# A hybrid encoder layer on one core: Fourier transforms in pieces between the projection's blocks, and the final norm during the last expert's down projection

## The chip, the cores and the metric

The kernel is one program on 1 core of one Trainium2 chip. The metric is the device time of one execution in microseconds; lower is better. A core has five engines with their own instruction streams: TensorE (PE; PEld is its weight load), VectorE (DVE), ScalarE (ACT), GpSimd (POOL) and SyncE (SP). They are ordered by semaphores alone. SP and POOL also issue the DMAs, which move data between main memory and the on-chip memory.

## The reference

Two batches of rows go through the same layer, 1024 rows ("prompt") and 256 ("sample"), each of width 1024. The kernel stacks them to T = 1280 rows, ten tiles of 128.

```
h = rmsnorm(x, norm_mix);  u = h @ w_in                 # w_in is 1024 x 2048
u_b, u_c, u_x, u_f = split(u)                           # 512 columns each
y_conv = rmsnorm(u_b * conv3(u_c * u_x), g_conv)        # 3 taps along the rows
y_four = rmsnorm(real(fft2(u_f over rows and over groups of 64 columns)), g_fourier)
x = x + concat(y_conv, y_four) @ w_out                  # 1024 x 1024
h = rmsnorm(x, norm_ffn)
aff = softmax(h @ w_router);  each of 16 experts takes its top rows (128 prompt, 32 sample)
ye = (silu(h_e @ w_gate[e]) * (h_e @ w_up[e])) @ w_down[e] * gate   # hidden width 2816
x[rows of e] += ye
out = rmsnorm(x, norm_final)
```

All of it is float32. Most products are made of three matmuls: each operand is split into a high part (rounded) and a low remainder, and high x high, high x low and low x high are added.

## The kernel before

**Projection.** Each 128-row tile of x is squared and summed (ACT, L566), scaled by its norm (DVE, L795), turned by TensorE (L1140), and split into `hT_h` (ACT, L576) and `hT_l` (DVE, L803). When all ten tiles are there, 16 blocks of 128 output columns follow. A block loads 128 columns of `w_in` (SP), scales and splits them into `win_h` (ACT, 8 instructions, L586) and `win_l` (DVE, 8 instructions, L810), and runs 72 matmuls (L1150) into one of two sets of three PSUM banks. The order is 12 blocks for the convolution and then 4 for the Fourier half. A block's consumer frees its banks for the block after the next.

**Fourier half.** After each of its four blocks ACT copies the second half of the rows (L612), DVE makes sums and differences (`tc`, L854), and both are split into `AB_h` (L615) and `AB_l` (L856). After the last block come "channels": per row tile 12 matmuls against the table `dd`, and a split of the 1024 columns into `Y_h` (ACT, L624) and `Y_l` (DVE, L865). Then come the "waves", for j = 0 to 3: 24 matmuls for the even frequencies, 24 for the odd ones and 12 for the sample rows, against the tables `tab_h`, `tab_l`, `tsm`. ACT copies the sines (`qcp`, L642), and DVE adds and subtracts (`yfour`, L883 to L895). `w_out` is loaded and split in halves of its rows' tiles between the waves, through two small buffers `wo_raw` (L632, L873). POOL squares and adds for the norms.

**Rows.** For each of the ten tiles `half` runs 24 + 24 matmuls with the two halves of `w_out`; DVE adds them to x, the norm is taken, and the router's logits are made. Results go to `acc_dram` (x) and `xn_dram` (its norm). Top-k runs on DVE beside and behind it. After `routed` POOL gathers the first expert's rows.

**Experts.** Weights come in 33 units of 1 MB per expert (22 for gate and up, 11 for down) through 11 slots. ACT writes `spl_h` (L704) and DVE `spl_l` (L1060) three units ahead of TensorE; a unit of the prompt is 12 matmuls. Sample rows are multiplied unsplit at five places of an expert (L1336, L1344), the last two behind the 7th and the 11th down unit. At an expert's end ACT scales the results by the gate (`yP`, `yS`), and POOL adds them into `acc_dram` by an indirect DMA.

**Final norm.** After the last expert all ten tiles are read from `acc_dram` (L461), normed (ACT L780 and L782, DVE L1126 and L1128) and written (L464).

The order is written out by hand in each engine's stream; an engine takes its instructions strictly in that order. The lines above are those of the profile.

Of the kernel before, what the change touches and what calls it, by code (L numbers as in the profile page):

```python
# [19 lines left out]
P = 128  # L20
# [8 lines left out]
E = 16  # L29
# [31 lines left out]
HALF = SEQ // 2  # L61
GROUPS = ((0, 4), (4, 8), (8, TILES))
EARLY = 4
# [8 lines left out]
def build(nc, x, norm_mix, w_in, conv_w, g_conv, g_fourier, w_out, norm_ffn, w_router, w_gate, w_up, w_down,  # L72
# [8 lines left out]
    out_t = out.rearrange("(t p) d -> t p d", p=P)  # L81
    win_v = w_in[0].rearrange("(k p) e -> p k e", p=P)

    win_v2 = w_in[0].rearrange("(k p) (a j l c) -> j p k a l c", p=P, a=4, j=2, l=2)
# [5 lines left out]
    with ExitStack() as ctx:  # L90
# [13 lines left out]
        Y_h = at("Y_h", 0, [P, JH, TILES, 2 * P], F32R)  # L104
        Y_l = at("Y_l", 40 * KB, [P, JH, TILES, 2 * P], F32R)
        yconv = at("yconv", 80 * KB, [P, JH, T])
        AB_h = at("AB_h", 100 * KB, [P, JH, T], F32R)
        AB_l = at("AB_l", 120 * KB, [P, JH, T], F32R)
# [11 lines left out]
        uc = at("uc", 164 * KB, [P, T])  # L120
        v = at("v", 169 * KB, [P, VW])
        tc = at("tc", 175 * KB, [P, T + 2])
        qc = at("qc", 181 * KB, [P, T])
        sqc = at("sqc", 186 * KB, [P, T])

        woc_h = at("woc_h", 140 * KB, [P, JH, D], F32R)
        woc_l = at("woc_l", 156 * KB, [P, JH, D], F32R)
        tab_h = at("tab_h", 172 * KB, [P, HB, LARGE], F32R)
        tab_l = at("tab_l", 172 * KB + HB * LARGE * 4, [P, HB, LARGE], F32R)
        tsm = at("tsm", 100 * KB, [P, 2, SMALL], F32R)  # L130
        qf = at("qf", 103 * KB, [P, T])
        sqf = at("sqf", 108 * KB, [P, T])
        qcp = at("qcp", 113 * KB, [P, HE + HO + SE + SO])
        wo_raw = at("wo_raw", 116 * KB, [P, 2, DH])

        wof_h = at("wof_h", 0, [P, JH, D], F32R)
# [10 lines left out]
        A0 = at("A0", 100 * KB, [E, HALF])  # L147
        A1 = at("A1", 102 * KB, [48, HALF])
        v0 = at("v0", 104 * KB, [E, CAP])
        v1 = at("v1", 104 * KB + 512, [48, CAP])  # L150
        i0 = at("i0", 105 * KB, [E, CAP], U32)
        i1 = at("i1", 105 * KB + 512, [48, CAP], U32)
        i0f = at("i0f", 106 * KB, [E, CAP])
        i1f = at("i1f", 106 * KB + 512, [48, CAP])
# [57 lines left out]
        def bank(b, n=1):  # L212
            return psf[:, b * 512:(b + n) * 512]

        const_in = sem("const_in")
        gffn_in = sem("gffn_in")
        dd_in = sem("dd_in")
        tab_in = sem("tab_in")
# [1246 lines left out]
```

## Time and profile before

| | us |
|---|---|
| median of 3 runs | 2580.14 (2579.91 to 2581.01) |
| the profiled execution's own time | 2579.22 |
| its span, first to last instruction | 2577.3 |
| TensorE busy in the span | 2438.6 (95%) |
| VectorE busy | 1650.2 (64%) |
| ScalarE busy | 1344.1 (52%) |
| GpSimd busy | 194.7 (8%) |
| mean granted clock of TensorE | 0.972 of full speed |

Full speed of TensorE is 2.4 GHz; the other level is half of that. All times in the text are positions or lengths within the span. The busy share alone does not tell what a stage is worth: 2438.6 of 2577.3 us are busy, and what can be won without fewer matmuls lies in the idle stretches and in those at the lower clock.

### The profile page before, as it was taken

The page shows a single profiled execution, that of the slowest core. Times are in us where ns is not written, and L with a number is a line of the kernel's source. Part 1 is how long each engine was busy: PE and PEld are TensorE (multiplying, and loading weights), DVE is VectorE, ACT ScalarE, POOL GpSimd, SP SyncE. Part 2 cuts the span into 40 slices and gives each one's busy share as a digit, 9 for nine tenths or more (in the row PEclk, how much of TensorE's full clock was granted, in tenths as well). Part 3 has the DMA queues.
Part 4 walks back from the last instruction along what each step waited for, and adds up shares of the span by engine and source line. Part 5 has one row for each costly group of instructions (what it writes and reads, how often), then busy time and mean ns, then how long its engine had stood idle before and what let it go on. Part 6 is the DMA issues. An engine that isn't in the chain of part 4 may idle for free.

```text
span 2577.3 us, 45156 instructions
## 1 busy us (share of the span) xinstructions
PE 2438.6 (95%) x18269; PEld 1915.0 (74%) x18269; DVE 1650.2 (64%) x1350; ACT 1344.1 (52%) x1233; POOL 194.7 (8%) x191
## 2 busy tenths in 40 slices
PE   5999879759999999999999999999999999999994
PEld 4888768647777777777777777777777777777773
DVE  4344455967676767667676666676767676666674
ACT  5222322325555556556555555565656565556563
POOL 0010120010101010101010101001010101010000
PEclk8999889879999999999999999999999999999997
DMA  3110242426878786868787878787877878787866
GB/s 119 41 33 25 99 168 107 173 98 258 317 264 316 269 299 262 298 261 299 279 305 280 307 280 307 279 309 269 313 275 285 301 264 322 266 320 267 318 261 222
DMA packets 296891, 627.28 MB, mean 243 GB/s; under 512 B 21392, under 2 KB 72848, under 8 KB 296464
## 3 DMA queue, kind: packets, MB, share of 16 engines
q1 hardware_dynamic: 288336, 598.88, 63.1%
q0 software_dynamic: 8384, 25.71, 3.7%
q8 instruction: 157, 2.57, 0.4%
q14 instruction: 14, 0.11, 0.0%
HBM read 598.31 MB, written 26.21 MB: 242 GB/s over the span
## 4 chain that ended last, share of the span: by engine, by line
PE 90%; DVE 5%; DMA 2%; ACT 1%; issue 1%; SPq 0%; POOL 0%; DVEq 0%; ACTq 0%; POOLq 0%
PE ps L353 20%; PE ps L354 19%; PE ps L355 19%; PE ps L1336 12%; PE ps L1150 9%; PE ps L1344 6%; PE ps L1354 1%; DVE i L935 1%; DVE v L933 1%; DVE A L937 1%; DMA raw<-in_w_gate_dram 1%; PE ps L1295 1%; DMA wo_raw<-in_w_out_dram 1%; DVE wof_l L873 0%; PE ps L1363 0%
## 5 line engine op out<-in xcount | busy, mean ns | idle before, releaser
L1060 DVE TENSOR_TENSOR spl_l<-raw,spl_h 128x2048 fp32r<-128x2048 f32 x528 | 1209.3, 2292 | 553.5 <-ACT spl_h L704 548.4
L704 ACT ACTIVATE spl_h<-raw 128x2048 fp32r<-128x2048 f32 x528 | 1012.1, 1917 | 576.5 <-PE ps L355 447.3
L353 PE MATMUL ps<-spl_h,xT 128*128 128x512 f32 x1408 | 555.0, 394 | 3.2 <-DVE xT L1065 2.5
L354 PE MATMUL ps<-spl_l,xT 128*128 128x512 f32 x1408 | 549.8, 390 | 0.0
L355 PE MATMUL ps<-spl_h,xT 128*128 128x512 f32 x1408 | 548.8, 390 | 0.0
L353 PEld LDWEIGHTS ps<-spl_h,xT 128*128 128x128 f32 x1408 | 264.7, 188 | 78.8 <-issue 22.3
L1336 PE MATMUL ps<-raw,xTs 128*32 128x256 f32 (+1 forms) x6144 | 314.2, 362 | 0.0
L355 PEld LDWEIGHTS ps<-spl_h,xT 128*128 128x128 f32 x1408 | 264.8, 188 | 56.1
L354 PEld LDWEIGHTS ps<-spl_l,xT 128*128 128x128 f32 x1408 | 264.8, 188 | 53.3
L353 PE MATMUL ps<-spl_h,g 128*128 128x512 f32 x704 | 278.0, 395 | 0.0
L354 PE MATMUL ps<-spl_l,g 128*128 128x512 f32 x704 | 274.4, 390 | 0.0
L355 PE MATMUL ps<-spl_h,g 128*128 128x512 f32 x704 | 274.3, 390 | 0.0
L1336 PEld LDWEIGHTS ps<-raw,xTs 128*32 128x32 f32 x6144 | 189.4, 110 | 109.7 <-issue 8.1
L538 POOL DMA_INDIRECT acc_dram<-yP,sidx x16 | 26.7, 1669 | 1797.1 <-ACT yP L745 1797.1
L353 PEld LDWEIGHTS ps<-spl_h,g 128*128 128x128 f32 x704 | 132.1, 188 | 40.0 <-issue 13.2
L1344 PE MATMUL ps<-raw,gs 128*32 128x256 f32 x2816 | 158.6, 380 | 0.0
L355 PEld LDWEIGHTS ps<-spl_h,g 128*128 128x128 f32 x704 | 132.2, 188 | 28.2
L354 PEld LDWEIGHTS ps<-spl_l,g 128*128 128x128 f32 x704 | 132.2, 188 | 26.6
L1344 PEld LDWEIGHTS ps<-raw,gs 128*32 128x32 f32 x2816 | 88.2, 110 | 63.3 <-issue 8.3
L1150 PE MATMUL ps<-hT_h,win_h 128*128 128x512 f32 (+1 forms) x384 | 96.6, 360 | 5.9 <-DVE win_l L810 5.9
L1150 PE MATMUL ps<-hT_l,win_h 128*128 128x512 f32 (+1 forms) x384 | 96.3, 359 | 0.0
L1150 PE MATMUL ps<-hT_h,win_l 128*128 128x512 f32 (+1 forms) x384 | 96.2, 359 | 0.0
(199 smaller groups left out, 1961.5 us busy)
## 6 DMA issues: line engine op xcount, KB each, us to landing
raw<-in_w_up_dram SPq DMA_DIRECT2D x352, 512.0 KB, 8.3
raw<-in_w_gate_dram SPq DMA_DIRECT2D x352, 512.0 KB, 9.6
raw<-in_w_down_dram SPq DMA_DIRECT2D x176, 1024.0 KB, 14.9
win_raw<-in_w_in_dram SPq DMA_DIRECT2D x16, 512.0 KB, 3.8
xt<-in_x_dram SPq DMA_DIRECT2D x10, 512.0 KB, 8.3
xr<-in_x_dram SPq DMA_DIRECT2D x10, 512.0 KB, 4.0
acc_dram<-xr SPq DMA_DIRECT2D x10, 512.0 KB, 2.6
xn_dram<-xn SPq DMA_DIRECT2D x10, 512.0 KB, 2.9
```

What stands on the lines that cost most here:

```text
L353: eng.matmul(o, a_h, b_h, start=first, stop=False, skip_group_check=True)
L354: eng.matmul(o, a_h, b_l, start=False, stop=False, skip_group_check=True)
L355: return eng.matmul(o, a_l, b_h, start=False, stop=last, skip_group_check=True)
L538: pool.indirect_dma_start(acc, bass.IndirectOffsetOnAxis(sidx[:, 0:1], 0), yP[:, :], None, compute_op=ALU.add).then_inc(added[0], 16)
L704: act.activation(spl_h[:, i % SPL, :], raw[:, slot_of(i), :], ACT.Copy).then_inc(sh_ok, 1)
L933: dve.max(v[0:n, rs], A[0:n, :]).then_inc(top_ok[h], 1)
L935: dve.max_index(idx[0:n, rs], v[0:n, rs], A[0:n, :]).then_inc(top_ok[h], 1)
L937: dve.match_replace(A[0:n, :], v[0:n, rs], A[0:n, :], -2.0).then_inc(top_ok[h], 1)
L1060: dve.tensor_tensor(spl_l[:, i % SPL, :], raw[:, slot_of(i), :], spl_h[:, i % SPL, :].bitcast(F32), ALU.subtract).then_inc(sl_ok, 1)
L1150: last = pe.matmul(u[:, t0:t1], w[:, slot, k, :], h[:, k, t0:t1], start=(k == 0 and i == 0), stop=(k == KD - 1 and i == 2), skip_group_che ...
L1336: last = pe.matmul(o, xTs[:, k, :], v_, start=k == 0, stop=k == KD - 1, skip_group_check=True)
L1344: last = pe.matmul(bank(6)[q * CAPS:(q + 1) * CAPS, 0:DQ], gs[:, f, :], raw[:, slot_of(i), b * D + q * DQ:b * D + (q + 1) * DQ], start=f = ...
```

## The change

1. **The start.** SP issues x's first tile and the weights of block 0 ahead of the small constants. The blocks are reordered: the four Fourier blocks are 0 to 3, the twelve convolution blocks 4 to 15. Blocks 0 and 1 run in pieces of rows (0:512, 512:1024, 1024:1280), and TensorE turns tiles 4 to 9 between their matmuls.
2. **Fourier pieces.** After the eight steps k of block n, TensorE runs `waves` of Fourier block n-3 (k = 0, 1, 2) and `channels` of block n-2 (k = 3 to 7). `Y` and `AB` shrink to what one or two blocks need. ACT and DVE work through the same loop over n. The tables are loaded at the start.
3. **w_out** is loaded whole: its first half during blocks 10 to 14, its second half after step 3 of block 15.
4. **Norm sums.** POOL makes the squares and sums of the Fourier half after block 6, TensorE sums them in block 10; ACT makes the squares of the convolution half.
5. **Experts' first loads.** Three units instead of four are loaded ahead of the rows; unit 7 and those behind it wait for `routed`. The first gather reads `idxT` directly, without the two copies into `gidx`.
6. **The final norm.** During the last expert's down projection all rows are read from `acc_dram` (which holds experts 0 to 14), normed and written to `out`, through five buffers and POOL's queue. The last expert's own rows are gathered ahead (`accP`, `accS`), get its result, are normed and overwrite their rows in `out` by two indirect DMAs at the end.

The core of the diff:

```diff
+FX = 5
+NORMS = {INS + 2: (0,), INS + 3: (1,), INS + 4: (2,), INS + 5: (3,), INS + 6: (4,), INS + 8: (5,), INS + 9: (6, 7),
+         INS + 10: (8, 9)}
-EARLY = 4
+EARLY = 3
...
 # SP
+            sp.dma_start(xt[:, 0, :], x_t[0]).then_inc(x_in[0], 16)
+            load_win(0)
+            for t in range(1, 5):
+                sp.dma_start(xt[:, t, :], x_t[t]).then_inc(x_in[t], 16)
+            load_win(1)
...
+            sp.wait_ge(hT_half, 1)
+            for k in range(JH):
+                sp.dma_start(wof_raw[:, k, :], wout_v[JH + k]).then_inc(wof_in[k // 2], 16)
...
             for i in range(EARLY, UNITS):
+                if slot_of(i) == 4:
+                    sp.wait_ge(routed, 1)
...
 # POOL, end
+            pool.wait_ge(xg_ps, E)
+            for t in range(3):
+                load_rows(t)
+            pool.wait_ge(pe_s, (E - 1) * SAMPLE + NC)
+            for t in range(3, FX):
+                load_rows(t)
+            for t in range(2):
+                store_rows(t)
+            for t in range(2, TILES):
+                if t + 3 < TILES:
+                    pool.wait_ge(f_out[(t + 3) % FX], 16)
+                    load_rows(t + 3)
+                store_rows(t)
+            for s in range(FX):
+                pool.wait_ge(f_out[s], 16 * len(range(s, TILES, FX)))
+            pool.wait_ge(z_ok, 1)
+            pool.indirect_dma_start(out, bass.IndirectOffsetOnAxis(sidx[:, 0:1], 0), accP[:, :], None).then_inc(z_out, 16)
+            pool.wait_ge(z_ok, 2)
+            pool.indirect_dma_start(out_q, bass.IndirectOffsetOnAxis(sidx[:, 1:2], 0), accS[:, :], None).then_inc(z_out, 16)
...
 # ACT
+            for n in range(1, PROJ):
+                if n <= JH:
+                    halves(n - 1)
...
+                if n + 1 < PROJ:
+                    win_hi(n + 1)
+                if n <= JH:
+                    sums_hi(n - 1)
...
+                if 3 <= n < 3 + JH:
+                    sines(n - 3)
+                if 2 <= n < 2 + JH:
+                    channels_hi(n - 2)
...
+            def row_norm(t):
+                act.wait_ge(f_in[t % FX], 16 * (t // FX + 1))
+                act.activation(bank(4, 2), fx[t % FX][:, :], ACT.Square, accum_out=fss[:, t:t + 1]).then_inc(fs_ok, 1)
+                act.wait_ge(fs_ok, t + 1)
+                act.activation(fss[:, TILES + t:TILES + t + 1], fss[:, t:t + 1], ACT.Sqrt, bias=eps[:, 0:1],
+                               scale=1.0 / D).then_inc(frt_ok, 1)
...
 # DVE, in expert(e, last), and behind the last expert
+                    if last:
+                        if i == 0:
+                            adder()
+                        for t in NORMS.get(i, ()):
+                            row_scale(t)
...
+            for k, (ps_, rows_, gain) in enumerate(((bank(0, 2), accP, gfin), (bank(6)[:, 0:DQ], accS, gfinq))):
...
+                dve.scalar_tensor_tensor(out=rows_[:, :], in0=ps_, scalar=cgate[:, k:k + 1], in1=rows_[:, :],
+                                         op0=ALU.mult, op1=ALU.add).then_inc(z_sum, 1)
+                dve.wait_ge(z_rt, k + 1)
+                dve.reciprocal(zrr[:, k:k + 1], zrt[:, k:k + 1]).then_inc(z_rr, 1)
+                dve.wait_ge(z_rr, k + 1)
+                dve.scalar_tensor_tensor(out=rows_[:, :], in0=rows_[:, :], scalar=zrr[:, k:k + 1], in1=gain[:, :],
+                                         op0=ALU.mult, op1=ALU.mult).then_inc(z_ok, 1)
...
 # PE
+            project(0, 0, 512, more_x({1: 4, 4: 5}))
+            pe.wait_ge(winl_ok, 2)
+            project(1, 0, 512, more_x({1: 6, 4: 7, 7: 8}))
+            pe.wait_ge(hTl_ok, 8)
+            project(0, 512, 1024, more_x({2: 9}))
+            pe.wait_ge(hTl_ok, 9)
+            project(1, 512, 1024)
+            pe.wait_ge(hTl_ok, TILES)
+            project(0, 1024, T)
+            project(1, 1024, T)
...
+            def posts(n):
+                def after(k):
+                    if 3 <= n < 3 + JH and k < 3:
+                        waves(n - 3, k)
+                    if 2 <= n < 2 + JH and k >= 3:
+                        channels(n - 2, k - 3)
+                    if n == 10 and k == 3:
+                        pe.wait_ge(qf_ok, 1)
+                        norm_sums(qf, 16)
+                return after
```

`row_scale(t)` is a reciprocal and one scaling on DVE, as L1126 and L1128 were; `adder` builds a 128 x 128 matrix of 32 x 32 identities, with which one matmul adds the four quarters of a sample row's sum of squares. In the order lists below, "waits" names the semaphores.

TensorE behind the last projection block, before:

```order
L1150 MATMUL ps<-hT_h,win_l 128x512 x2
L1150 MATMUL ps<-hT_h,win_l 128x256
L1180 MATMUL ps<-ones,qc 128x1 [waits q_ok]
L1180 MATMUL ps<-ones,qc 128x1 x9
L353 MATMUL ps<-dd,AB_h 128x256 [waits abl_ok,dd_in]
L354 MATMUL ps<-dd,AB_h 128x256
L355 MATMUL ps<-dd,AB_l 128x256
```

TensorE of the change, where block 2 ends and block 3 begins (`dd` is a channels piece, `tab` a piece of waves):

```order
L380 MATMUL ps<-dd,AB_l_56 128x256
L1297 MATMUL ps<-hT_h,win_h 128x512 [waits ab_ok,winl_ok]
L1297 MATMUL ps<-hT_h,win_h 128x512
L1297 MATMUL ps<-hT_h,win_h 128x256
L1297 MATMUL ps<-hT_l,win_h 128x512 x2
L1297 MATMUL ps<-hT_l,win_h 128x256
L1297 MATMUL ps<-hT_h,win_l 128x512 x2
L1297 MATMUL ps<-hT_h,win_l 128x256
L378 MATMUL ps<-tab_h,Y_h 128x258 [waits tab_in,Yl_ok]
L379 MATMUL ps<-tab_l,Y_h 128x258
```

The pieces stood behind all blocks; now each stands behind 9 of a block's 72 matmuls.

VectorE in block 3 of the change, up to the first waves:

```order
L918 TENSOR_TENSOR sums<-ps,tmp 128x512 [waits abl_ok,tmp_ok]
L918 TENSOR_TENSOR sums<-ps,tmp 128x512
L918 TENSOR_TENSOR sums<-ps,tmp 128x128 x2
L891 SCALAR_TENSOR_TENSOR win_l<-win_raw,gmix,win_h 128x128 [waits winh_ok]
L891 SCALAR_TENSOR_TENSOR win_l<-win_raw,gmix,win_h 128x128 x7
L922 TENSOR_TENSOR AB_l_56<-sums,AB_h_54 128x1280 [waits abh_ok]
L937 TENSOR_TENSOR yfour<-ps,qcp 128x257 [waits qcp_ok]
L938 TENSOR_TENSOR yfour<-ps,qcp 128x255
```

Before, the `yfour` pair stood behind the channels' splits alone; now a block's sums and weight split stand ahead of it.

VectorE in the last expert's down projection, before:

```order
L1060 TENSOR_TENSOR spl_l<-raw,spl_h 128x2048 [waits sh_ok] x7
L1088 TENSOR_TENSOR g<-ps,g 128x4x128 [waits gh_ok]
L1060 TENSOR_TENSOR spl_l<-raw,spl_h 128x2048 [waits sh_ok]
L1126 RECIPROCAL frr<-fss 128x1 [waits frt_ok,gfin_in]
L1128 SCALAR_TENSOR_TENSOR fo<-fx,frr,gfin 128x1024 [waits fr_ok]
```

And in the change (`fx_125` and `fx_126` are two of the five row buffers):

```order
L1180 TENSOR_TENSOR spl_l<-raw,spl_h 128x2048 [waits sh_ok]
L1214 RECIPROCAL frr<-fss 128x1 [waits frt_ok]
L1216 SCALAR_TENSOR_TENSOR fx_125<-fx_125,frr,gfin 128x1024 [waits fr_ok]
L1180 TENSOR_TENSOR spl_l<-raw,spl_h 128x2048 [waits sh_ok]
L1208 TENSOR_TENSOR g<-ps,g 128x4x128 [waits gh_ok]
L1214 RECIPROCAL frr<-fss 128x1 [waits frt_ok]
L1216 SCALAR_TENSOR_TENSOR fx_126<-fx_126,frr,gfin 128x1024 [waits fr_ok]
```

A row tile's scaling now stands between two splits of weights.

## Rows read from the trace of the kernel before

**Rows 1.** Windows: length, busy time (instructions) by engine, granted clock, DMA share, GB/s

```profile
43.44:270.77 227.33, 227.33 (x1155) 192.95 (x1155) 84.44 (x159) 49.76 (x129) 21.09 (x8) 0.99 0.11 33
270.77:301.39 30.62, 19.77 (x139) 18.34 (x138) 15.55 (x16) 12.44 (x14) 3.03 (x4) 0.87 0.44 164
301.39:351.57 50.18, 33.32 (x240) 32.42 (x241) 32.02 (x50) 15.91 (x34) 19.57 (x8) 0.81 0.33 107
...
2541.40:2577.30 35.90, 0.00 (x0) 0.00 (x0) 13.76 (x20) 15.31 (x32) 1.55 (x1) 0.56 0.90 325
```

**Rows 2.** Timeline of the start: start, length, engine, line, output and inputs, count

```profile
4.08 5.13 SPq L370 DMA_DIRECT2D xt<-in_x_dram  x10
...
22.91 1.02 ACT L576 ACTIVATE hT_h<-ps 128x1024 fp32r<-128x1024 f32 x1 [0.48 <-PE ps L1140]
...
31.31 1.09 PE L1140 MATMUL ps<-ident,xs 128*128 128x128 f32 x8 [0.91 <-DVE xs L795]
...
38.55 4.76 ACT L586 ACTIVATE win_h<-win_raw,gmix 128x128 fp32r<-128x128 f32 x16
...
41.11 4.43 DVE L810 SCALAR_TENSOR_TENSOR win_l<-win_raw,gmix,win_h 128x128 fp32r<-128x128 f32 x16 [1.20 <-ACT win_h L586]
```

**Rows 3.** Chain of waits, 270 to 360 us: start, length, what

```profile
271.57 1.70 DVE tc L854 x4
273.29 1.28 ACT AB_h L615
274.59 1.50 DVE AB_l L856
...
307.04 0.40 ACT qcp L642
307.46 0.43 DVE yfour L883
...
358.69 2.12 PE ps L1180 x20
```

**Rows 4.** Timeline of TensorE: first matmuls of two neighbouring sets of waves

```profile
310.87 0.37 PE L353 MATMUL ps<-tab_h,Y_h 128*128 128x258 f32 x1
...
317.90 0.37 PE L353 MATMUL ps<-tab_h,Y_h 128*128 128x258 f32 x1
```

**Rows 5.** Windows, a stretch during the waves, columns as in Rows 1

```profile
326.00:331.00 5.00, 5.00 (x30) 5.00 (x31) 5.00 (x4) 1.08 (x3) 4.90 (x2) 0.66 0.32 102
```

**Rows 6.** TensorE's waits from 270 to 352 us: total, times, longest

```profile
PE ps L353 <- DVE Y_l L865: 3.2, 4, 0.8
```

**Rows 7.** Timeline around the first gather

```profile
533.42 2.26 POOL L518 COPY gidx<-idxT 128x1 uint32<-128x1 uint32 x1 [179.19 <-DVE gateT L1055]
...
543.85 1.94 PE L1295 MATMUL ps<-ident,xg 128*128 128x128 f32 x8 [10.90 <-DMA xgs<-xn_dram,gidx]
```

**Rows 8.** Timeline of VectorE and ScalarE in the last down projection

```profile
2516.35 2.29 DVE L1060 TENSOR_TENSOR spl_l<-raw,spl_h 128x2048 fp32r<-128x2048 f32 x1 [0.42 <-ACT spl_h L704]
...
2517.12 1.92 ACT L704 ACTIVATE spl_h<-raw 128x2048 fp32r<-128x2048 f32 x1 [0.80 <-PE ps L355]
```

**Rows 9.** Chain of waits, 2500 us to the end

```profile
2520.40 6.18 PE ps L1344 x112
...
2542.66 5.27 DMA acc_dram<-yS,sidx
...
2555.47 1.16 ACT fsq L780 x2
2556.65 0.30 ACT fss L782
2557.17 1.28 DVE fo L1128
```

**Rows 10.** Transfers: count, KB each, median us from issue to landing

```profile
tsm<-in_dft_s_dram POOLq DMA_DIRECT2D x1, 260.0 KB, 4.0
...
xgs<-xn_dram,gidx POOLq DMA_INDIRECT x16, 7.7
```

More of the change, by code:

```diff
@@ new lines, in wo_lo @@
+            def wo_lo(n):
+                dve.wait_ge(woh_ok, n + 1)
+                k = n % JH
+                full, hi, lo = ((woc_raw, woc_h, woc_l) if n < JH else (wof_raw, wof_h, wof_l))
+                dve.scalar_tensor_tensor(out=lo[:, k, :], in0=full[:, k, :], scalar=gm2[:, n:n + 1],
+                                         in1=hi[:, k, :].bitcast(F32), op0=ALU.mult, op1=ALU.subtract).then_inc(wol_ok, 1)
+            for n in range(1, PROJ):
+                if n <= JH:
+                    sums_of(n - 1)
+                j, q = divmod(n - 1 - JH, 3)
+                if n > JH and q == 1:
+                    gated(j)
+                if n > JH and q == 2:
+                    conv_out(j)
+                if n + 1 < PROJ:
+                    win_lo(n + 1)
+                if n <= JH:
+                    sums_lo(n - 1)
+                if n > JH and q == 1:
+                    taps(j)
+                if 3 <= n < 3 + JH:
+                    waves(n - 3)
+                if 2 <= n < 2 + JH:
+                    channels_lo(n - 2)
+                if n == 11:
+                    dve.wait_ge(rn_rt, 1)
+                    dve.reciprocal(rn[:, 1, :], rm[:, 1, :]).then_inc(rn_a, 1)
+                if n == 14:
+                    for k in range(JH):
+                        wo_lo(k)
@@ L1184, in _ @@
[L1184 to L1195 removed]
+                    if n == PROJ - 1 and k == JH - 1:
+                        last.then_inc(hT_half, 1)
@@ new lines, in project, with channels @@
+                    if k == KD - 1 and t1 == T:
+                        last.then_inc(u_done, 1)
+                    if between is not None:
+                        between(k)
+            def channels(j, p):
+                if p == 0:
+                    pe.wait_ge(abl_ok, j + 1)
+                    if j:
+                        pe.wait_ge(yf_ok, 8 * j)
+                    else:
+                        pe.wait_ge(dd_in, 16)
+                if p >= 2:
+                    pe.wait_ge(Yl_ok, PIECES * j + p - 1)
+                for i in range(2):
+                    ts = slice((2 * p + i) * P, (2 * p + i + 1) * P)
+                    last = three(pe, bank(6 + p % 2)[:, i * 2 * P:(i + 1) * 2 * P], AB_h[j % 2][:, ts], AB_l[j % 2][:, ts],
@@ L1410, in _ @@
             expert(E - 1, True)
+            pe.wait_ge(same_ok, 2 * QS - 2)
+            pe.wait_ge(z_sq, 2)
+            pe.matmul(bank(7)[:, 0:1], same[:, :], zss[:, 1:2], start=True, stop=True).then_inc(z_ps, 1)
 def split12(a):
```

672 lines of the change are left out of this document (362 added, 310 removed).

## The prediction

> **What bounds the kernel now.** I read the windows by stage first, then the chain of waits where a window shows idle time, then the timeline there for durations. The windows [rows 1] show four kinds of stage. The 16 projection blocks run without a gap, 227.3 us or 14.2 a block, with VectorE and ScalarE at 84 and 50 us. The channels (30.6 us) have TensorE busy 19.8 us, and the waves with the loading of `w_out` (50.2 us) 33.3 us, at a granted clock of 0.87 and 0.81. After the last matmul 35.9 us pass without TensorE. The stage of the rows, the top-k and experts 0 to 14 are the same work in both kernels. So three places count: the start and Fourier half (0 to 351.6 us), the first gather, and the end. The total matmul work stays.
>
> **The start.** x's first tile is issued at 4.08 us [rows 2]; with only one small transfer ahead it goes out near 1.3, 2.8 us earlier. ScalarE then makes block 0's `win_h` ahead of the tiles: half of 4.76, 2.4 us [rows 2], which gives that back. Tile 3's `hT_h` ended at 23.9 us; it stays near 23.6, and VectorE, with half of 4.43 us for `win_l`, about 1.5 of it in idle time, ends tile 3's `hT_l` near 26.5. There the first projection piece starts, instead of at 43.4. Blocks 0 and 1 are 28.2 us of matmuls (227.3 less about 2 for the slow beginning, over 16: 14.08 a block), the six tiles turned between them take 1.1 us each at the high clock [rows 2], 7 with their hand-offs, and the slow first microseconds cost 1.7, as a first run of matmuls does here: both end near 63.4.
>
> A wait is added: block 2's `win_h` needs block 0 finished, and block 0 ends only 2.8 us (24 matmuls of 256 columns at 0.118) ahead of block 1. From 60.6 on: ScalarE's copy of halves 0.8, `win_h` 2.4, `win_l` 2.2, hand-offs 0.4. Block 2 starts at 66.5; TensorE stands 3 us.
>
> **The Fourier pieces.** From 66.5: 14 blocks at 14.08 are 197.1; channels, 120 matmuls at 0.12, are 14.4; waves, four sets at 7.03 (310.87 to 317.90) [rows 4], are 28.1; one norm sum is 2.1 [rows 3]. What each piece waits for follows from the hand-offs, in block 3 counted from its first matmul. ScalarE ends the last channels copy at 0.7, the halves at 1.5, `win_h` at 3.9, `AB_h` (1.28) at 5.2, and then takes the sines (0.40). VectorE ends the sums (1.70) at 3.2, `win_l` at 6.2, `AB_l` (1.50) at 7.8, and the first `yfour` pair (0.43 and 0.33) at 8.6 [rows 3]. TensorE comes to the second waves piece at 1.76 + 2.95 + 1.76 = 6.5, so it waits 2.2 us. All behind that is covered: the third piece's needs are ready 1 us early, and a channels piece has 1.76 us of matmuls against 1.3 of splitting. The same in block 4; 0.9 us in block 5, which has no sums; 2.6 in block 6, where the gated product and taps stand ahead. Together 7.9 us. Queued behind the waiting matmul are only the block's own; nobody else is late, since blocks 3 to 5 last 25 to 27 us and the other engines need under 14.
>
> Do these waits cost clock? Four waits of 0.8 us in the channels [rows 6] left the clock high, but a stretch of the waves with single waits around 1 us in it shows 0.66 [rows 5]. The bounds are 0 and one slow stretch behind each of five waits at 1.7, 8.5 us; I take 4.6, half way.
>
> Block 15 ends at 66.5 + 197.1 + 14.4 + 28.1 + 2.1 + 7.9 + 4.6 = 320.7. Then VectorE's last convolution product, the copy of the first row tile and its low part, 3.5 us: `half` starts at 324.2. Before it started at 351.57 [rows 1]. Gain 27.4 us. `w_out`'s transfers and splits are off the path: 2 MB are issued 7 us ahead, and the second half's splits (8.1 us on ScalarE behind block 15) end before `half`, the norm sum and their 3.5 us are over at 12.7. Bounds: 18 (all waits double, clock lost at each) and 37 (no wait, no clock lost).
>
> The Trainium skill has a rule on this tail. "SBUF — State Buffer", section Who interferes with whom, says that a VectorE instruction with two inputs in this memory blocks a GpSimd instruction that reads it, and the other way round, for its whole length. GpSimd's last sum of squares would by it stand against the splits of `w_out` behind block 15. By the rule one of them is up to 3 us later, still inside the 12.7; the sum would lose 0 to 1 us. The next paragraph's rows agree with the rule.
>
> **The first gather.** GpSimd copies two index columns at 533.42, 2.26 us each, and TensorE gets its rows at 543.85 [rows 7]. The change drops both copies, 4.5 us, and a hand-off of 0.9. But four units, 4 MB, are now requested at that very moment; under such load the second gather takes 7.7 us to land [rows 10], against about 3.7 here (10.4 us from 533.42 to 543.85, less 4.5 and 0.9, less 1.3 until the second of two gathers is issued). 5.4 less 4.0 is 1.4; without any collision 5.4. I take 3. Unit 7 is split only after four units' work; its 4 MB are in 15 us after the request: no wait.
>
> **The end.** In the last down projection a unit lasts 2.72 us; ScalarE works 1.92 and idles 0.80, VectorE 2.29 and idles 0.42 [rows 8]. A row tile adds 1.16 + 0.30 + 0.1 on ScalarE and 1.28 + 0.17 + 0.15 on VectorE [rows 9]. VectorE then needs 3.9 us a unit over five units, TensorE 2.72. The three split buffers give 1.1 us of lead and TensorE stops behind the 7th down unit for the sample rows' 6.18 us [rows 9]: following units 3 to 7 through, TensorE loses 1.05 us once and catches the rest there. The transfers are free, as all weights are in by then.
>
> What ends last? Row tiles 0 to 4 are ready at 2515.0, 2519.2, 2523.0, 2526.8 and 2531.3, tiles 5 to 8 from 2535.8 to 2540.4. Tile 9 uses tile 4's buffer: store from 2531.5, load, then norm. A transfer of 512 KB on POOL's queue is not in the trace; 260 KB took 4.0 us [rows 10], so I take 4.8, with 3.2 and 8.4 as bounds. Store to 2536.3, load to 2541.9, ScalarE 1.55, VectorE 1.6: tile 9 is ready at 2545.0, 2.6 us behind TensorE's end (2541.4 + 1.05). Now `accP`, queued behind it on VectorE: sum 1.28, square 1.25, root 0.3, reciprocal 0.17, scaling 1.28, hand-offs 0.3: 2549.6. `accS`: 0.4 + 0.65 + 0.5 + 0.3 + 0.2 + 0.45 and hand-offs, 2552.7. The last scatter 5.27 us [rows 9]: 2558.0, end 2558.4. Before 2577.3. Gain 18.9 us, bounds 14 and 24.
>
> The Trainium skill gives a fit for such a transfer ("DMA: Bandwidth & Descriptors", section Anatomy of one DMA): 2.0 us plus bytes over 436 GB/s, 3.2 us for 512 KB. This trace disagrees: 260 KB took 4.0 where the fit says 2.6. By the fit the end would come about 3 us earlier, near 2528.
>
> **Sum.** 27.4 + 3 + 18.9 = 49.3. The profiled execution took 2579.2 (span 2577.3), so 2529.9; it lies 0.9 under the median of the runs, so 2531.
>
> **Rivals.**
> A. The pieces never make TensorE wait long enough to matter: 7.9 + 4.6 + 3 fall away, 2515. For it: every wait is a difference of sums of small hand-offs. Against: VectorE's order puts three items ahead of `yfour`.
> B. Slower than before. In blocks 2 to 6 TensorE stops in every block, and the granted clock stays at its low level through them. Their work at the high clock is 5 x 14.08 + 14.4 + 28.1 = 113 us; all of it at half clock costs 113, giving 2644. It turns to a loss once 44% of that stretch is slow. For it: 0.66 in [rows 5], 0.81 over the waves. Against: 0.8 us waits kept the clock, and here 25 us of dense work stand between two waits.
> C. The final rows are late. If POOL's transfers take 8.4 us, the two in tile 9's chain add 7.2 and the scatters 3: 2541.
> D. The start doesn't overlap: ScalarE and VectorE, not TensorE, pace the pieces up to 63 us, and the blocks of the convolution wait too. Adds 10: 2541.
>
> **How the numbers follow.** My case 0.62, A 0.13, B 0.04, C 0.11, D 0.10. The likeliest gives 2531. The range reaches to A (2515) and past C and D with their own spread: 2514 to 2548; only B and a joint C and D lie outside. Only B ends slower: 0.04. For no change 49 us would have to vanish exactly: 0.01. This kernel's runs agree within 0.05%, so that 0.2% (5 us) can be told.
>
> **What would show it.** The first projection matmul at 26 to 27 us; block 2 at 66 after a 3 us wait for `win_l`; a wait of about 2 us for `yfour` in blocks 3, 4 and 6, none in the convolution blocks; `half` near 324; the gap before the first gathered rows shorter by 3 us; one wait of about 1 us in the last down projection; 16 to 17 us from TensorE's last matmul to the end instead of 36. I am wrong if waits of over 1 us appear in channels pieces or in blocks 7 to 15, if the clock falls under 0.9 in blocks 3 to 6, or if the rows or experts 1 to 14 change their pace.

## The result

The changed kernel takes 2585.8 us (median of 16 runs, 2582.2 to 2590.7), the kernel before 2580.5 (2579.4 to 2581.2, 16 runs): ratio 1.0022, 95% interval 1.0014 to 1.0029. It is slower, by 5 us, where the forecast was 49 us faster, with 0.04 on slower. The profiled execution took 2586.2 us (span 2584.3).

### The profile after

The page of the changed kernel: busy tenths in 40 slices, and the queues (packets, MB, share of the DMA engines).

```profile
span 2584.3 us, 44975 instructions
PE   6999999299999999999999999999999999999997
PEclk8999999599999999999999999999999999999998
...
q8 instruction: 160, 2.62, 0.4%
```

TensorE is at 9 from the second slice on, but for the eighth, where it waits for the top-k in both kernels: the front is as dense as it was meant to be. The timeline of TensorE at the places that the prediction priced (start, length, instruction, idle time before and its releaser), against [rows 1, 7]:

```profile
25.98 0.76 PE L1297 MATMUL ps<-hT_h,win_h 128*128 128x512 f32 x1 [2.46 <-DVE hT_l L905]
...
64.81 0.85 PE L1297 MATMUL ps<-hT_h,win_h 128*128 128x512 f32 x3 [2.54 <-DVE win_l L891]
...
92.14 0.39 PE L378 MATMUL ps<-tab_h,Y_h 128*128 128x256 f32 x1 [1.61 <-DVE yfour L938]
...
322.42 0.76 PE L378 MATMUL ps<-woc_h,ysh 128*128 128x512 f32 x1 [3.89 <-DVE ysl L1017]
...
514.82 1.94 PE L1467 MATMUL ps<-ident,xg 128*128 128x128 f32 x8 [11.16 <-DMA xgs<-xn_dram,qidxT]
```

`half` begins at 322.42 (before 351.57, forecast 324.2), the first gathered rows are turned at 514.82 (before 543.85): 29.0 us are gained by then, all of it ahead of `half`: from there to the first gathered rows pass 192.4 us, before 192.3. The loss lies behind. Windows of TensorE (length, busy time, matmuls, granted clock, DMA share, GB/s), from the first gathered rows to the end, first of before, then of after:

```profile
543.85:2577.30 2033.45, 1994.24 (x15904) 0.99 0.78 283
```

```profile
514.70:2584.30 2069.60, 2012.81 (x15906) 0.99 0.77 279
```

The same matmuls take 36 us longer, though the end in them was to be 19 us shorter: 55 us are missing. TensorE's waits in the changed kernel (total, times, longest) name them:

```profile
PE ps L379 <- issue: 31.5, 13, 2.6
...
PE ps L378 <- DVE yfour L938: 6.7, 4, 2.8
...
PE ps L378 <- issue: 3.5, 1, 3.5
...
PE ps L1297 <- DVE win_l L891: 2.7, 2, 2.5
```

"issue" is time in which no semaphore was waited for. There are fourteen such stalls, one after each of the 13 jumps back in the loop over experts 1 to 14, and one of 3.5 us where the loop is left. TensorE's timeline at one of them (the row L1516 is the last of an expert, the rows behind it the first of the next):

```profile
769.67 0.61 PE L1516 MATMUL ps<-raw,gs 128*32 128x256 f32 x8
770.21 0.50 PE L378 MATMUL ps<-spl_h,xT 128*128 128x512 f32 x1
...
772.38 0.39 PE L378 MATMUL ps<-spl_h,xT 128*128 128x512 f32 x1
775.22 0.50 PE L379 MATMUL ps<-spl_l,xT 128*128 128x512 f32 x1 [2.44 <-issue]
775.55 0.55 PE L380 MATMUL ps<-spl_h,xT 128*128 128x512 f32 x1
775.90 0.63 PE L378 MATMUL ps<-spl_h,xT 128*128 128x512 f32 x1
776.32 0.63 PE L379 MATMUL ps<-spl_l,xT 128*128 128x512 f32 x1
```

The tenth matmul after the jump is the last (all 13 stalls stand ahead of L379), then TensorE stands 2.4 us, and then its matmuls follow each other at 0.43 us instead of 0.23: the clock is at its lower level (0.55 granted in the window 775.3 to 778.8). Before, the same place runs through:

```profile
796.71 3.66 PE L1344 MATMUL ps<-raw,gs 128*32 128x256 f32 x64
800.30 0.50 PE L353 MATMUL ps<-spl_h,xT 128*128 128x512 f32 x1
800.64 0.40 PE L354 MATMUL ps<-spl_l,xT 128*128 128x512 f32 x1
```

**Theory F**: TensorE waits for its own instructions. The Trainium skill says ("Runtime: NRT & Kernel Launch", Instruction fetch mechanics) that an engine's instructions are fetched in blocks of 16 KiB, 256 instructions, in order, and that a jump to a block that isn't there forces a fetch before execution goes on. This trace agrees with the size: 160 packets of the instruction queue moved 2.62 MB. The loop body has 2,058 instructions (994 matmuls in the trace of a turn, each with its loading of weights, and 70 others), a little over eight blocks, and the instruction queue moves nine packets in a turn (770.2 to 898.9). The loop itself is the same in both kernels, but the code ahead of it grew by 863 instructions: modulo 256 the loop's first instruction moved from 75 to 170 and its jump back from 85 to 180. The expectations below were written with another count. It takes a product of the sample rows as one matmul where the trace has two, and so has a body of 1,498 instructions, six blocks, and the jump 48 too early in its block; its origin is another (85 for 75). The shifts from run to run are right in it. **Rival P**: a hand-off or transfer that the change shifted (the unit loads, three early units instead of four).

### The profile page after: what moved, and what is told of

Read it like the earlier page. It is cut to its first block, busy times and chain, and to the rows that moved or that the text cites. A ratio compares the mean times of both kernels' runs of the same rounds, so it can differ in the third digit from the quotient of the medians.

```text
span 2584.3 us, 44975 instructions
## 1 busy us (share of the span) xinstructions
PE 2449.8 (95%) x18271; PEld 1917.9 (74%) x18271; DVE 1638.5 (63%) x1367; ACT 1346.8 (52%) x1243; POOL 155.9 (6%) x207
## 3 DMA queue, kind: packets, MB, share of 16 engines
q8 instruction: 160, 2.62, 0.4%
## 4 chain that ended last, share of the span: by engine, by line
PE 90%; DVE 4%; issue 3%; ACT 2%; DMA 1%; POOL 0%; SPq 0%; POOLq 0%; DVEq 0%; ACTq 0%
PE ps L378 21%; PE ps L379 20%; PE ps L380 20%; PE ps L1508 12%; PE ps L1297 8%; PE ps L1516 6%; PE ps L1526 1%; DVE i L1050 1%; DVE v L1048 1%; DVE A L1052 1%; ACT win_h L626 1%; PE ps L1467 1%; DVE win_l L891 1%; DMA raw<-in_w_down_dram 0%; PE ps L1535 0%
## 5 line engine op out<-in xcount | busy, mean ns | idle before, releaser
L379 PE MATMUL ps<-spl_l,xT 128*128 128x512 f32 x1408 | 556.6, 395 | 31.5 <-issue 31.5
L379 PEld LDWEIGHTS ps<-spl_l,xT 128*128 128x128 f32 x1408 | 268.2, 190 | 91.1 <-issue 37.0
L378 PEld LDWEIGHTS ps<-spl_h,xT 128*128 128x128 f32 x1408 | 267.8, 190 | 82.8 <-issue 26.2
L380 PEld LDWEIGHTS ps<-spl_h,xT 128*128 128x128 f32 x1408 | 268.1, 190 | 57.1
L379 PE MATMUL ps<-spl_l,g 128*128 128x512 f32 x704 | 274.5, 390 | 0.0
L1516 PE MATMUL ps<-raw,gs 128*32 128x256 f32 x2816 | 158.6, 380 | 0.0
L379 PEld LDWEIGHTS ps<-spl_l,g 128*128 128x128 f32 x704 | 132.2, 188 | 26.6
L1516 PEld LDWEIGHTS ps<-raw,gs 128*32 128x32 f32 x2816 | 88.2, 110 | 63.3 <-issue 8.3
L1297 PE MATMUL ps<-hT_h,win_h 128*128 128x512 f32 (+1 forms) x384 | 103.9, 366 | 5.2 <-DVE win_l L891 2.7
L1297 PE MATMUL ps<-hT_h,win_l 128*128 128x512 f32 (+1 forms) x384 | 102.5, 362 | 0.0
L1297 PE MATMUL ps<-hT_l,win_h 128*128 128x512 f32 (+1 forms) x384 | 102.3, 362 | 0.0
## 6 DMA issues: line engine op xcount, KB each, us to landing
raw<-in_w_down_dram SPq DMA_DIRECT2D x176, 1024.0 KB, 13.9
```

Of the source, the lines that this page charges most:

```text
L378: eng.matmul(o, a_h, b_h, start=first, stop=False, skip_group_check=True)
L379: eng.matmul(o, a_h, b_l, start=False, stop=False, skip_group_check=True)
L380: return eng.matmul(o, a_l, b_h, start=False, stop=last, skip_group_check=True)
L1297: last = pe.matmul(u[:, a:b], w[:, n % 2, k, :], h[:, k, a:b], start=(k == 0 and i == 0), stop=(k == KD - 1 and i == 2), skip_group_check= ...
L1516: last = pe.matmul(bank(6)[q * CAPS:(q + 1) * CAPS, 0:DQ], gs[:, f, :], raw[:, slot_of(i), b * D + q * DQ:b * D + (q + 1) * DQ], start=f = ...
```

## The experiments

Each ran beside the kernel before on the same chip (its medians 2580.2 to 2581.0); ratios are to it, with 95% intervals.

### The place of the loop

```diff
+            for _ in range(64):              # before_pad94: 94, in the kernel before
+                pe.sem_inc(lone, 1)
             gathered(1)
             expert(0, False)
```

**after_pad64.** 

> The changed kernel with 64 semaphore increments (on a semaphore that nobody waits for) put into TensorE's stream just before its code for expert 0, so that the loop over experts 1 to 14 begins 64 instructions later in the stream; nothing else differs, and nothing is left out. Theory F (the stall of 2.4 us per expert ten matmuls after the jump back is TensorE waiting for its own instructions, and it depends on where the loop's first instruction lies): the 13 stalls and the half-clock stretch of 3 us behind each go, 14 x 4 us: 2530 us (2525 to 2538), ratio to before 0.980. Rival P (the stall is a hand-off or transfer, the unit loads or the slots' order with three early units): the padding changes nothing but 64 short instructions, some 2 us: 2586 to 2588 us, ratio 1.002.

**before_pad94.** 

> The kernel before with 94 such increments at the same place, which puts its loop's first instruction where the changed kernel has it, counted in instructions and modulo 256. Nothing is left out. Theory F: the stall appears here too, 14 times 2.4 us and 1.6 us of clock: 2580 + 55 = 2635 us (2620 to 2640), ratio 1.021. Rival P: 2581 to 2583 us, ratio 1.001.

Measured: `before_pad94` 2631.7 us, ratio 1.0197 (1.0180 to 1.0214). The kernel before, with nothing but 94 idle instructions, takes the changed kernel's stall, of the same length behind the same tenth matmul. That is what F forecast (2635), and it rules P out. (94 leave the loop one instruction short of the changed kernel's place.) The increments themselves were on the path for 3.0 us of it (TensorE's wait ahead of the first gathered rows is 13.9 us, before 10.9), which leaves 48 for the place of the loop.

```profile
804.03 0.39 PE L353 MATMUL ps<-spl_h,xT 128*128 128x512 f32 x1
806.87 0.40 PE L354 MATMUL ps<-spl_l,xT 128*128 128x512 f32 x1 [2.45 <-issue]
```

`after_pad64` took 2601.2 (1.0081, 1.0064 to 1.0098), worse, not 2530. My F was too simple: the stall was now 3.6 us, at the jump itself (769.6 to 773.2). With 64 more, the jump lies only 48 instructions behind the beginning of a block (where I had placed the beginning itself), so it, too, needs its distance.

**front_pad64** (the end of before put back, 64 increments). 

> The changed kernel with the end of before (its start, Fourier pieces and first gather kept) and the 64 increments ahead of TensorE's expert 0. Nothing is left out. Prediction's terms: 27.4 + 3 gained, 2550 us; by the changed kernel's trace (gather transposes 29.1 us earlier) and theory F: 2551.5 us, ratio 0.9887. Rival P (the stall comes with the three early units of the changed start): 2551 + 55 = 2606 us.

Measured 2615.9 (1.0140): the same stalls (46.3 us in 13). It says nothing on its own term; see front_pad162.

**after_pad12.** 

> The changed kernel with 12 increments: the loop's first instruction lies 12 instructions nearer to its block's end. Nothing is left out. Theory F: the stall comes after 4 matmuls instead of 10 (a matmul is two instructions) and is longer by these 6 x 0.23 us: 3.8 us each, 14 x 1.4 = 19 us over the changed kernel, 2604 us, ratio 1.009. Rival P2 (the stall's place in the loop is set by data): ten matmuls after the jump as in the changed kernel, 2586 us.

Measured 2620.8 (1.0155, 1.0139 to 1.0170), 17 us over the forecast. The stall grew, as F says, but by 2.1 us where 1.4 was forecast, and lay ahead of the first matmul and not behind the fourth. So the place of the block's end is known to some ten instructions only.

**after_pad162.** 

> The changed kernel with 162 idle semaphore increments at TensorE's expert 0. Nothing is left out. Theory F, mended by what 64 of them did (the 2.4 us stall ten matmuls after the jump became one of 3.6 us at the jump itself, 2601 us; and the kernel before took the changed kernel's stall with 94 of them): TensorE's instructions come in blocks of 256, and a loop is free of stalls only if its first instruction has enough of its block ahead of it and its jump enough of its block behind it. Modulo 256 the kernel before has its loop's first instruction at 85 and its jump at 47; 162 more instructions put the changed kernel's there too. So no stalls: 2530 us (2526 to 2538), ratio 0.981. Rival P2 (the stalls come with the changed order of the unit loads and only their length depends on the place): 2585 to 2600 us.

Measured 2550.2 (0.9880, 0.9865 to 0.9895). Not one stall at the loop is left. But the increments themselves were on the path: TensorE's `L1467 <- issue` ahead of the first gathered rows was 24.6 us (before the gather itself held it 11.2), 0.15 us for each. 2550.2 less the 13.4 is 2536.8.

**after_split** (98 of the 162 ahead of `pe.wait_ge(pick_ok, 7)`, where TensorE idles 24.4 us). 

> The changed kernel with 162 idle increments as in after_pad162, but 98 of them ahead of the wait for the top-k's picks (TensorE idles 24.4 us there) and 64 ahead of the first gathered rows (11.2 us idle). An increment takes 0.15 us: 162 in one place took 24.6 us and put 13.4 us on the path. Nothing is left out. Theory F: 2550.2 less 13.4: 2537 us (2533 to 2541), ratio 0.983. Rival (a stall of another kind fills the place): 2550 us.

Measured **2536.4** (2535.1 to 2538.0), ratio 0.9826 (0.9813 to 0.9840). The kernel is the changed one, computes all that it does, and is 44 us faster than before. The same window as above (it begins 0.8 us ahead of the first gathered rows, which come at 513.84):

```profile
513.00:2534.50 2021.50, 1996.63 (x15906) 0.99 0.78 286
```

From the first gathered rows on that is 48.8 us less than in the changed kernel: 35.0 of stalls and 16.2 of busy time at the lower clock, less 2.4 that other gaps add.

Three more kernels look at the rule itself.

```diff
-            with nc.Fori(1, E - 1, engines=(pe.engine,), hint_back_edge=True) as e:
+            with nc.Fori(1, E - 1, engines=(pe.engine,), hint_back_edge=False) as e:
```

**split100.** 

> As after_split with 100 increments in all instead of 162: the loop's first instruction moves 62 instructions towards its block's beginning, and the jump with it. Nothing is left out. Theory F: with 64 the jump lay at a block's very beginning and TensorE stood 3.6 us at it; here it lies 36 instructions in, 18 sample matmuls of 0.057 us or 1.0 us, so that the stall should be 2.6 us, all of it at the jump: 14 x 4.1 over after_split, 2594 us (2570 to 2600). Rival (only a bad place at the loop's beginning stalls, and 64 was bad for another reason): 2536 us.

**split210.** 

> As after_split with 210 increments in all: the loop's first instruction lies 48 nearer to its block's end, the jump 48 deeper in its own. Nothing is left out. Theory F with what the runs so far gave (a block's packet moves 2.1 us after it is asked for, and its instructions run 3.1 us after that, 5.2 in all): from the first instruction to the block's end some 72 instructions are left, about 30 matmuls of 0.23 or 7 us, more than 5.2, so that nothing stalls: 2537 us (2534 to 2541). Rival (only the very place of the kernel before is good): 14 stalls of some 2 us with their clock, 2570 us or more.

Measured: split_nohint 2630.5 (1.0197), just over the forecast's 2608 to 2629, with a stall of 5.3 us at each of the 13 jumps:

```profile
764.28 3.66 PE L1518 MATMUL ps<-raw,gs 128*32 128x256 f32 x64
773.23 0.69 PE L378 MATMUL ps<-spl_h,xT 128*128 128x512 f32 x1 [5.28 <-issue]
```

split100 2566.5 (0.9949), stalls of 2.2 us ahead of the first matmul; the forecast was 2594, since I had taken 1.5 us of lost clock for each, and here the matmuls behind the shorter stall keep 0.23 us. (The profile puts these stalls down to `DVE spl_l`. But the split that it names, 770.3 to 772.6, is one that the first matmul does not need: in after_split that matmul runs at 769.5, while the same split still runs, 769.4 to 771.7.) split210 2540.8 (0.9846): no stall at the loop, as forecast; of its 4 us over after_split, `DVE spl_l` waits are 8.0 us in 8 against 3.7 in 5; the rest is open.

The transfers show the mechanism directly. In windows of half a microsecond, the instruction queue's row (packets, MB, share of 16 engines) appears only where a block is fetched. First split_nohint, 770.0 to 770.5; the changed kernel, 772.5 to 773.0; after_split, 763.0 to 763.5:

```profile
q8 instruction: 1, 0.02, 13.7%
```

```profile
q8 instruction: 1, 0.02, 14.1%
```

```profile
q8 instruction: 1, 0.02, 13.9%
```

| kernel | last matmul of an expert ends | packet | TensorE goes on |
|---|---|---|---|
| split_nohint | 767.9 | 770.0 | 773.2, at the first matmul |
| after_pad64 | 769.6 | 770.0 | 773.2, at the first |
| split100 | 770.8 | 770.0 | 773.0, at the first |
| changed | 770.2 | 772.5 | 775.2, at the eleventh |
| after_split | 769.5 | 763.0, and 771.5 | no stall |

From a packet's half microsecond to the first instruction of its block pass 2.7 to 3.2 us, and without the hint the packet moves 2.1 to 2.6 us after the last matmul: 5.3 us from needing to having. This is in a stretch where the units' loads hold the DMA engines (share 1.05). With the hint, the target's block moves ahead of the jump, once TensorE comes into the block with the jump. In after_split the jump lies 146 instructions behind that block's beginning, which are 72 matmuls and 5.5 us, so that the block is entered near 764.0, and the packet is at 763.0. In split100 it lies 84 behind it, 42 matmuls of 0.057 us or 2.4 us: entered near 768.4, packet at 770.0, too late. So some 5 us are needed here too. The block behind the target's moves only after the jump (771.5, 772.5), and must be there when the target's is used up. All places tried, with the block's end put at 196 modulo 256, where the changed kernel's stall has it:

| loop's first instruction to its block's end | block's beginning to the jump | stall |
|---|---|---|
| 120 (after_split, the other runs with 162; before, within one) | 146 | none |
| 72 (split210) | 194 | none |
| 26 (changed; before_pad94, within one) | 240 | 2.4 us |
| 14 (after_pad12) | 252 | 4.5 us |
| 218 (after_pad64, front_pad64) | 48 | 3.6 us |
| 182 (split100) | 84 | 2.2 us |

Not every loop is fetched again. The kernel before has a second one on TensorE, two turns over the convolution blocks of 878 instructions each. It moved three packets in its first turn (between 44 and 94 us) and none in its second (none from 94 to 212), while the long loop moves nine in every turn. Where between 878 and 2,058 instructions the bound lies, no run shows.

### The front and the gather

**front_pad162.** 

> The changed kernel with the end of before and the 162 increments. Nothing is left out. Theory F: start, Fourier half and gather alone give 29 us: 2551 us (2548 to 2555), ratio 0.9887; by the prediction's terms 2549.7. Rival P2: 2605 us or more.

Measured 2564.8 (0.9935, 0.9921 to 0.9948), with the increments' 13.4 us on the path as in after_pad162, which I had not foreseen: 2551.4 without them. That is 29.6 us under before, forecast 30.4 by the prediction's terms and 29 by the trace.

The gather's copies put back:

```diff
-            pool.indirect_dma_start(xg[:, :], None, xn_d, bass.IndirectOffsetOnAxis(idxT[:, 0:1], 0)) ...
-            pool.indirect_dma_start(xgs[:, :], None, xn_q, bass.IndirectOffsetOnAxis(qidxT[:, 0:1], 0)) ...
+            gather(0, None)
```

**pad162_copies.** 

> As after_pad162, but the first gather copies its two index columns first, as before (the third part of the change undone). Nothing is left out. The prediction's term: 3 us slower than after_pad162, bounds 1.4 and 5.4. From the changed kernel's trace (the first gather now takes 2.9 us to be issued and 7.1 to 9.7 us to land, TensorE waits 11.2 us for it, before 10.9): if the unit loads that start at the same moment slow the gather whatever it does, the copies add their whole 5.4 us; if the copies only let the loads get ahead, 0 to 1.4 us.

**split_copies.** 

> As after_split, but the first gather copies its two index columns first, as before (in pad162_copies the increments themselves ended last, so that one could not tell). Nothing is left out. Prediction's term: 3 us slower than after_split (1.4 to 5.4): 2540 us. From the changed kernel's trace, if the unit loads slow the gather whatever it does: 5.4 us slower; if the copies only let the loads get ahead, 0 to 1.4.

pad162_copies took 2548.5 and tells nothing: the increments ended later than either gather. split_copies took 2539.0 (2536.4 to 2543.9) against 2536.4: 2.6 us, within the runs' spread but confirmed by TensorE's wait, first of after_split, then of split_copies:

```profile
PE ps L1469 <- DMA xgs<-xn_dram,qidxT: 11.1, 1, 11.1
```

```profile
PE ps L1467 <- DMA xgs<-xn_dram,gidx: 13.8, 1, 13.8
```

That is 2.7 us of the 5.4 that the copies take. Of the rest, 1.9 us went to GpSimd's issuing of the first gather, which took 2.9 us in after_split and 1.0 in split_copies; why, no run shows. From its issue to its landing the second gather took 7.1 us and 6.5, before 3.6: with the copies or without them, it is slower in the changed kernel.

**split_hold** (`sp.wait_ge(xg_in[0], 16)` and `[1]` ahead of the fourth unit's load). 

> As after_split, but the queue of weights waits, ahead of the fourth unit, until the first gather has landed, so that no unit load shares the DMA engines with it. Nothing is left out. Collision theory (the loads cost the gather what the dropped copies gave): the landing falls from 7.1 us to about 3.7, 3 to 4 us faster than after_split, 2533.5 us, if units 3 to 6 are still in time. Rival (a gather takes 7 us by itself, and the estimate of 3.7 in the prediction was wrong): no change, or slower by the later loads.

Measured 2537.4 (0.9825), as after_split. But the second gather's transfer fell from 7.1 to 3.7 us (508.2 to 511.9; in after_split 506.6 to 513.7), as the collision theory has it. TensorE then waited for the increments (9.3 us, "issue"; first gathered rows at 513.6 against 513.8), so that the gain could not reach the total. What it would be worth without them is open.

### The end

**before_end** (the changed end in the kernel before; TensorE's loop stays where it was). 

> The kernel before with the end of the changed one alone (final norm of the rows during the last expert, accP and accS); the start, the Fourier half and the first gather are those of before, and TensorE's stream ahead of and in the loop is the same. Prediction's term: 18.9 us gained, bounds 14 and 24: 2561.5 us, ratio 0.9927. Reading of the changed kernel's trace (POOL's loads of rows and the last weights get in each other's way, ScalarE waited 3.8 us for weights there, the end 17 us after the last matmul): 13 to 16 us gained, 2566 us, ratio 0.9945. Under theory F and under rival P no stall per expert: TensorE's loop as before. Should the stall come with the end's code after all, 2615 us.

Measured 2566.2 (0.9946, 0.9930 to 0.9963): 13.9 us gained, of 18.9 forecast, and no stall at the loop. In after_split, the window of the last down projection, and the one behind it (with ScalarE's busy time):

```profile
2474.00:2496.00 22.00, 16.85 (x17) 1.00 1.02 411
2496.00:2520.00 24.00, 13.62 (x25) 0.99 0.75 267
```

The DMA engines are full until 2496: eight loads of 1 MB of weights, and two of rows among them. ScalarE waited 2.90 us for the sixth down unit:

```profile
2482.89 1.92 ACT L782 ACTIVATE spl_h<-raw 128x2048 fp32r<-128x2048 f32 x1 [2.90 <-DMA raw<-in_w_down_dram]
```

and the chain of waits at the end goes over tile 9's load, as forecast, but at 5.66 us where 4.8 stood in the sum. This load comes 14 us after the last weights are in, among other rows' loads and stores:

```profile
2511.07 5.66 DMA fx<-acc_dram
...
2516.75 1.16 ACT ps L820 x2
...
2519.66 1.29 DVE accP L1272
...
2525.54 0.99 POOL out_dram L602
```

Four kernels tried to mend it.

```diff
 split_late:    + pool.wait_ge(sl_ok, (E - 1) * UNITS + INS + 6)   # ahead of load_rows(3)
 split_six:     - FX = 5
                + FX = 6    # sixth buffer at 108 KB, over sv and pv[0]; its load waits for p_ok and pT_ok
 split_sprows:  the stores and load_rows(5 to 9) written in sync's block, same waits
```

**split_sprows.** 

> As after_split, but the stores of the final rows and the loads of row tiles 5 to 9 are issued by SyncE's queue and not GpSimd's (the first five loads and the last two scatters stay with GpSimd). Nothing is left out. Theory Q (transfers of 512 KB on GpSimd's queue take 5.5 to 6.5 us here, those of SyncE's queue 2.6 to 4.0, and tile 9's store, load, store chain ends last): three of them shrink by 2 to 3 us each, of which the last matmul's own chain (accP, accS) lets 5 to 6 through: 2531.5 us. Rival (the transfers are slow because of what else moves then, whatever the queue): 0 to 1 us faster.

**split_late.** 

> As after_split, but the loads of row tiles 3 and 4 wait until six of the last expert's eleven down units are split. Nothing is left out. Theory W (two loads of 512 KB share full DMA engines with the last 8 MB of weights and make ScalarE wait 2.9 us for the sixth down unit, and everything behind it is late by that): the wait goes, 2.7 us faster than after_split, 2533.7 us. Rival (VectorE's 3.6 us a unit bind there anyway, and the rows come too late for their norms): 0 to 1 us.

**split_late6.** 

> As split_late, with a sixth buffer for rows (where sv and a third of pv lie, which are done by then), so that tile 9 takes tile 3's buffer and not tile 4's. Nothing is left out. Theory B (tile 9's chain of store, load, norm, store ends last): its load starts 5 us earlier, of which about 4 reach the end: 2529.5 us, with split_late's 2.7 in it. Rival (the transfers share one bandwidth, so that an earlier one only makes others later; moving them to SyncE's queue gained nothing): 0 to 1 us over split_late.

**split_six.** 

> As split_late6, but row tiles 3 and 4 are loaded as early as in the changed kernel (and tile 5 with them): the sixth buffer alone. Nothing is left out. If the sixth buffer gave the 2.6 us: 2534 us. If the later loads did (against what split_late says, which was even): 2536.5 us. If both edits are needed together, since a third early load makes ScalarE wait longer for weights (2.9 us with two): 2537 to 2538 us.

Measured, beside after_split's 2536.4: split_sprows 2539.3 (0.9832, 0.9819 to 0.9845), not faster where theory Q had 5 us of gain, and tile 9's load still 6.30 us: the queue is not what makes it slow. split_late 2536.6 (0.9834): ScalarE's wait for weights is gone, and waits of 6.5 us for `fx` stand in its place. split_late6 2533.8 (0.9822), split_six **2532.8** (2531.3 to 2533.6), ratio 0.9813 (0.9800 to 0.9827), the fastest of all. So the sixth buffer gives 3 to 4 us and the later loads nothing. Theory B had most of its price; W's 2.7 us did not come, as the time that ScalarE no longer waits for weights it waits for rows.

## Why the prediction was wrong

**The step that failed** is the sentence "The stage of the rows, the top-k and experts 0 to 14 are the same work in both kernels. So three places count". The work is the same; where its instructions lie in the stream is not. No term of the sum was for it, and no rival named it. It costs 49 us, 2585.8 less 2536.4, shown twice: by before_pad94, which has it without the change (51, of which 3 are the increments' own), and by after_split, which has the change without it. The last sign that I gave for being wrong, that experts 1 to 14 change their pace, is what showed it.

**The start and the Fourier pieces** (27.4) held at every step that I priced: first projection matmul 25.98 (forecast 26.5), block 2 at 64.81 after 2.5 us (66.5 after 3), waits for `yfour` 6.7 us in four (7.9), `half` at 322.4 (324.2). The clock was 0.97 in blocks 2 to 4 and 1.00 in the next two (windows 66 to 119 and 119 to 170), so that even my 4.6 us for it were too many. The gain at `half` was 29.1. Rivals B and D are out. So is A by its waits, which took 6.7 us, but the clock cost nothing, as A had it.

**The gather** (3): nothing. TensorE waited 11.2 us for its first rows, before 10.9, and the forecast sign "the gap before the first gathered rows shorter by 3 us" did not come. Of the 5.4 us that the copies had taken, the collision took 3.5 (7.1 us from issue to landing against 3.6; its full price stood at 4.0), and GpSimd's issuing of the first gather took 1.9 (2.9 us against 1.0), for which the sum had nothing. Dropping the copies is worth 2.6 us, but only against the changed kernel with the copies (split_copies). That start, pieces and gather together were forecast at 30.4 and came to 29.6 (front_pad162 less its increments) is luck, two errors of opposite sign.

**The end** (18.9, bounds 14 and 24): 13.9, just under the lower bound. Two terms of it were mis-sized: TensorE's loss in the last expert, and the way from its last matmul to the end. "The transfers are free, as all weights are in by then" was wrong: [rows 8] show ScalarE waiting for TensorE, not for weights, and I took that for idle DMA engines; in the same stretch of before their share is 1.03 (a window with VectorE's busy time):

```profile
2514.00:2518.00 4.00, 3.58 (x2) 1.00 1.03 411
```

With them full, the loads of row tiles 3 and 4 took 7.6 and 9.8 us (after_split), and the last weights came in at 2496.8. Behind that, among other rows' transfers, tile 9's load took 5.7 to 6.3, not 4.8. (The sum's step from 2536.3 to 2541.9 has 0.8 us more than that load, which it doesn't name.) From the first gathered rows to TensorE's last expert matmul are 2002.4 us in after_split against 1997.5 before, 4.9 lost where I had 1.05; from there to the end 18.2 us (forecast 16.0, before 35.9). Rival C, transfers at 8.4 us, had the right kind of error; its size was too large.

The front with the gather, and the end: 29.6 + 13.9 = 43.5 us, measured 44.4 without the stalls. The sum would have stood at 2536, five over the forecast, had the loop kept its place.

## What to carry to other kernels

Where code is added or taken away ahead of a long loop on a busy engine, compare the loop's place modulo 256 instructions before and after (count matmuls as the trace has them, not as the source has), and look for "issue" rows of equal length, once per turn, at the jump or a few matmuls behind it. Idle instructions put where the engine waits anyway move the loop for nothing; here 162 of them were worth 49 us, and between 72 and 120 instructions to the block's end, with the jump 146 to 194 behind its block's beginning, were safe. And a wait for another engine doesn't say that the DMA engines are free: read their share before a transfer is called free.

## What the hardware showed that I had not expected

- A pure change of place costs 2.4 us at each turn, and the 14 stalls, 35 us in all, take 16 us more through the clock: after 2.4 us of standing, 9 matmuls ran in 3.5 us where 17 do; after 2.2 us (split100) none was slow.
- A block of instructions is there 5.3 us after it is needed, of which some 3 pass after its packet has begun to move (shown with the DMA engines full; with idle ones it wasn't tried).
- The hint on the jump back is worth 94 us here (2630.5 against 2536.4).
- A loop of 878 instructions fetched nothing in its second turn; one of 2,058 moved nine blocks in every turn.
- The gather's transfer took 7.1 us beside loads of weights and 3.7 without them (after_split, split_hold).
- An idle semaphore increment takes TensorE 0.15 us (162 in 24.6).
- Two loads of 512 KB moved from a full stretch to a later one gained nothing (2536.6 against 2536.4).
